# Last layer normalisation of a hybrid attention and mixture-of-experts block: tokens loaded and stored in pairs of tiles

## The reference, cut to what matters

```
def layer_norm(x, g, b):
    xf = x.astype(jnp.float32)
    mu = jnp.mean(xf, -1, keepdims=True)
    var = jnp.mean(jnp.square(xf - mu), -1, keepdims=True)
    y = (xf - mu) * lax.rsqrt(var + LN_EPS)
    return (y * g.astype(jnp.float32) + b.astype(jnp.float32)).astype(x.dtype)
...
    h = layer_norm(DN_ALPHA * h + ffn, ln2_g[l], ln2_b[l])
return h[:, N_META:]
```

## Time and profile before

| what | value |
|---|---|
| median of 3 runs | 2524.76 us (2520.92 to 2529.96) |
| the profiled execution's own time | 2522.01 us |
| its span, first to last instruction | 2519.9 us |
| instructions | 35973 |
| PE busy | 2200.0 us (87%) |
| DVE busy | 1700.5 us (67%) |
| ACT busy | 1504.0 us (60%) |
| POOL busy | 331.3 us (13%) |
| first instruction of `phase_combine` | 2462.9 us after the start of the span |

### The profile page before, as it was taken

How to read it: one execution, slowest core, us unless ns; L and a number is a source line. 1 busy time by engine, 2 the same in 40 slices (tenths; PEclk the granted TensorE clock), 3 DMA queues, 4 the chain that set the end, 5 groups by cost and what they waited for, 6 DMA issues and landing times. The chain is left out here.

```text
span 2519.9 us, 35973 instructions
## 1 busy us (share of the span) xinstructions
PE 2200.0 (87%) x11294; PEld 1783.4 (71%) x11294; DVE 1700.5 (67%) x3112; ACT 1504.0 (60%) x2389; POOL 331.3 (13%) x436
## 2 busy tenths in 40 slices
PE   7999899758859999999979995599999999999970
PEld 6778788635547777777858884487888888888860
DVE  5323231166658888888843333889999999999976
ACT  4323241266646777776743432477888888788866
POOL 0111111100000000000000000112222222222211
PEclk9999999979979999999989997799999999999995
DMA  6425352252252222211043331799878779999837
GB/s 196 174 100 157 121 180 84 75 133 77 68 129 66 66 68 68 68 39 36 9 149 134 145 137 59 255 368 322 270 239 274 251 250 316 326 313 300 272 93 283
DMA packets 210506, 420.06 MB, mean 167 GB/s; under 512 B 36264, under 2 KB 86776, under 8 KB 209496
## 3 DMA queue, kind: packets, MB, share of 16 engines
q1 hardware_dynamic: 177352, 314.15, 36.6%
q0 software_dynamic: 32016, 103.26, 14.2%
q10 hardware_dynamic: 1032, 1.31, 0.4%
HBM read 437.12 MB, written 86.39 MB: 208 GB/s over the span
## 5 line engine op out<-in xcount | busy, mean ns | idle before, releaser
L2343 DVE TENSOR_TENSOR moe_w_lo<-fetch_w_raw,moe_w_hi 128x1024 fp32r<-128x1024 f32 x376 | 435.4, 1218 | 12.1 <-ACT moe_w_hi L2272 11.9
L2272 ACT ACTIVATE moe_w_hi<-fetch_w_raw 128x1024 fp32r<-128x1024 f32 x376 | 369.1, 1053 | 75.7 <-DMA fetch_w_raw<-in_w_e_up_dram 39.2
L2397 PE MATMUL moe_ps_gu<-moe_w_hi,moe_xT_hi 128*128 128x512 f32 x736 | 293.2, 398 | 4.5 <-DVE moe_xT_lo L2354 4.5
L2399 PE MATMUL moe_ps_gu<-moe_w_hi,moe_xT_lo 128*128 128x512 f32 x736 | 288.9, 393 | 0.0
L2398 PE MATMUL moe_ps_gu<-moe_w_lo,moe_xT_hi 128*128 128x512 f32 x736 | 288.5, 392 | 0.0
L1350 ACT ACTIVATE fox_p_hi<-fox_ps_t 128x512 fp32r<-128x512 f32 (+4 forms) x352 | 181.3, 531 | 108.5 <-PE fox_ps_t L1490 107.7
L1417 DVE TENSOR_TENSOR fox_p_lo<-fox_ps_t,fox_p_hi 128x512 fp32r<-128x512 f32 (+4 forms) x352 | 211.0, 611 | 28.8 <-ACT fox_p_hi L1350 27.3
L1490 PE MATMUL fox_ps_t<-ident,fox_s 128*128 128x128 f32 (+1 forms) x1216 | 200.0, 279 | 29.6 <-ACT fox_s L1343 18.7
L2349 DVE TENSOR_TENSOR moe_d_lo<-fetch_d_raw,moe_d_hi 128x1024 fp32r<-128x1024 f32 x184 | 213.0, 1221 | 10.3 <-ACT moe_d_hi L2280 10.1
L1404 DVE CUSTOM_DVE_ANT_0 fox_s<-fox_ps_r,fox_ncum 128x512 f32<-128x512 f32 (+4 forms) x352 | 193.7, 569 | 21.1 <-PE fox_ps_r L1475 14.0
L1343 ACT ACTIVATE fox_s<-fox_s,fox_ntop 128x144 f32<-128x144 f32 (+5 forms) x192 | 173.4, 904 | 46.8 <-DVE fox_ntop L1412 46.4
(11 more groups left out here) (312 smaller groups left out, 5002.9 us busy)
## 6 DMA issues: line engine op xcount, KB each, us to landing
fetch_w_raw<-in_w_e_gate_dram SPq DMA_DIRECT2D x192, 512.0 KB
fetch_w_raw<-in_w_e_up_dram SPq DMA_DIRECT2D x192, 512.0 KB
fetch_d_raw<-in_w_e_down_dram SPq DMA_DIRECT2D x92, 1024.0 KB
proj_w_raw<-in_w_in_dram SPq DMA_DIRECT2D x24, 1024.0 KB, 5.2
proj_xt<-in_x_dram SPq DMA_DIRECT2D x16, 512.0 KB
h<-proj_hrow POOLq DMA_DIRECT2D x16, 512.0 KB, 3.4
win_q_raw<-qT SPq DMA_DIRECT2D x32, 256.0 KB, 4.0
mix_o<-o SPq DMA_DIRECT2D x16, 512.0 KB, 4.4
```

Source lines behind the costliest of these rows:

```text
L2272: nc.scalar.activation(w_hi[:, k], w_raw[:, k].rearrange("p j n -> p (j n)"), ACT.Copy).then_inc(gu_high, 1)
L2343: nc.vector.tensor_tensor(w_lo[:, k], w_raw[:, k].rearrange("p j n -> p (j n)"), w_hi[:, k].bitcast(F32), ALU.subtract).then_inc(gu_split, 1)
L2397: nc.tensor.matmul(out, xT_hi[:, slot, k], w_hi[:, k, cols], start=k == 0, stop=False)
L2399: done = nc.tensor.matmul(out, xT_lo[:, slot, k], w_hi[:, k, cols], start=False, stop=k == KT - 1)
```

## The change

A pair of tiles (2 pair, 2 pair + 1) now has one load and one store of 1 MB instead of two of 512 KB. The slots stay as they were: four of `base` and four of `out`, pair 0 in slots 0 and 1, pair 1 in slots 2 and 3, and so on. SP has 8 loads, POOL 8 stores. The load of a pair waits until both tiles of the pair two before it have passed L2523. The store waits until both its tiles are finished. ACT waits, for either tile of a pair, on the pair's one semaphore, and DVE waits before L2523, for either tile, until the store of the whole pair two before has landed. The work of ACT and DVE on a tile is the same.

```
-        base_in = [m.sem(f"base_in{i}") for i in range(4)]
+        base_in = [m.sem(f"base_in{i}") for i in range(2)]
...
-        stored = [m.pool_dma_sem(f"stored{i}") for i in range(4)]
+        stored = [m.pool_dma_sem(f"stored{i}") for i in range(2)]
...
-            def load(n, slot, use):
-                wait(sp, normed, n - 3)
-                sp.dma_start(base[:, slot], t["acc"][n * P:(n + 1) * P, :]).then_inc(base_in[slot], 16)
-                if n == 0:
+            for pair in range(TILES // 2):
+                two = slice(2 * (pair % 2), 2 * (pair % 2) + 2)
+                wait(sp, normed, 2 * (pair - 1))
+                sp.dma_start(base[:, two], t["acc"][2 * pair * P:2 * (pair + 1) * P, :].rearrange("(j p) d -> p j d", p=P)
+                             ).then_inc(base_in[pair % 2], 16)
+                if pair == 0:
                     sp.dma_start(gain[:], row_broadcast(t["ln2_g"][0], P)).then_inc(const_in, 16)
                     sp.dma_start(shift[:], row_broadcast(t["ln2_b"][0], P)).then_inc(const_in, 16)
-
-            tiles(sp, load)
...
-            def store(n, slot, use):
-                pool.wait_ge(ready, n + 1)
-                pool.dma_start(t["out"][0, n * P:(n + 1) * P, :], out[:, slot]).then_inc(stored[slot], 16)
-
-            tiles(pool, store)
-            for i in range(4):
+            for pair in range(TILES // 2):
+                two = slice(2 * (pair % 2), 2 * (pair % 2) + 2)
+                pool.wait_ge(ready, 2 * (pair + 1))
+                pool.dma_start(t["out"][0, 2 * pair * P:2 * (pair + 1) * P, :].rearrange("(j p) d -> p j d", p=P),
+                               out[:, two]).then_inc(stored[pair % 2], 16)
+            for i in range(2):
                 pool.wait_ge(stored[i], 16 * TILES // 4)
...
-                act.wait_ge(base_in[slot], 16 * (use + 1))
+                act.wait_ge(base_in[slot // 2], 16 * (use + 1))
...
-                wait(dve, stored[slot], 16 * use)
+                wait(dve, stored[slot // 2], 16 * use)
```

## The result

The changed kernel takes 2533.5 us (median of 7 runs, 2528.98 to 2539.05) against 2524.76 us before. The ratio of the runs is 1.0034, with a 95% interval of 1.0020 to 1.0047. It is slower, by 8.7 us or 0.34%; 2534.0 was predicted. The interval reaches from 5 to 12 us, so the runs show that there is a loss, and not its size to a microsecond. The profiled execution took 2530.75 us, its span is 2528.7 us.

The account below looks back on a forecast made before the run. Last phase taken as lead-in, sixteen tiles at 2.64 us with ACT and DVE in step and DMA busy, lead-out. 1.55 + 6.3 + 0 + 1.35 = +9.2 us on 2524.76 made 2534.0; range 2527.7, rounded down, to 2541.

Parts of the forecast that it names:

- Part 1: Start of last phase: tile 0 waits for 1.049 MB, so ACT starts tile 1 later, +1.55 us (1.1 to 1.75).
- The cover of gain and shift: Start of last phase: gain and shift usable 1.5 us before DVE asks for them after ACT's root of tile 0.
- Part 2: Middle: pair loads take 5.9 us against 3.81 allowed, stalling ACT before pairs 2, 4, 6; +6.3 us (3.3 to 9.6).
- Part 2's aside on the size: Middle: half of each pair asks 2.64 us later and twice as much must come in the time left.
- Part 3: DVE's wait for stores before L2523: stores take 6.4 us against 7.4 us available, so it costs nothing.
- Part 4: End of last phase: last store moves 1.049 MB, +1.28 us, and POOL's issue +0.07; +1.35 us (1.28 to 1.5).
- Part 5: Vanished SP and POOL issues are worth nothing; tail with four fewer semaphores to reset, 0 to -0.3 us, taken 0.
- Busy all the time at 410 GB/s: Last phase before the change: the 16 DMA engines are always busy, leaving no rate for larger transfers to win.
- The pair's load nearly in time: First rival, ACT's L2505 of tiles 4, 8, 12: load takes 4.66 us, +5.4 us in sum; chance 0.23.
- Transfers queued one behind the other: Second rival, middle: loads take 7.5 us and DVE waits for stores too, sum 14.0 us; chance 0.14.
- The pattern of two pieces: Third rival, pair transfers: not spread over 16 engines, moving at half rate or below, about +21 us; chance 0.03.

Follow-up runs that it names:

- the kernel without stores: Changed kernel without the stores of pairs 0 to 6 and DVE's wait for them, output incomplete; phase 61.6 us, middle 46.0 us.
- The late-release run: Single 512 KB tiles as before, but both loads of a pair issued only at the pair's release point; ratio to before 1.0035, phase 65.5 us.
- the trimmed kernel: Kernel before, with root table loaded early, tile 1 loaded ahead of shift, last tile finished and stored in halves; ratio 0.9995, phase 55.7 us.
- pairs with eight slots: Changed kernel with eight input and eight output slots instead of four each; ratio to before 1.0014, phase 58.7 us.

## Why the prediction was right

The sum was +9.2 us on the profiled execution; it measured +8.7, of which 8.4 lie in the last phase. The medians, 2534.0 predicted and 2533.5 measured, agree more closely than they can tell: the interval of the ratio is 7 us wide, and the same kernel's phase measured +7.6 us in its second profile. The terms were off by -1.0, +0.7 and -0.5 us, and that they partly cancel is luck; that the middle carries the loss, by loads that miss ACT, is not. By its own steps:

**Part 1, the first load: the place was right, the size was not.** +1.55 us was predicted, with 1.1 as the lower bound; +0.58 was measured, below both. The step that failed is the reading of the stretches. I took the time at which 1.049 MB in total had moved as the time at which the pair's megabyte would be through, and assumed the same rates after the change: 270 GB/s until 2468. After the change, the stretch 2466 to 2468 runs at 418 GB/s and only the next at 317 (share and GB/s last):

```profile
2466.00:2468.00 2.00, 0.00 (x0) 0.00 (x0) 0.00 (x0) 0.00 (x0) 0.00 (x0) 0.50 1.04 418
2468.00:2470.00 2.00, 0.00 (x0) 0.00 (x0) 0.00 (x0) 1.44 (x3) 0.00 (x0) 0.50 0.96 317
```

In both kernels the slow stretch is the one in which the gain row should be on its way, the transfer behind the first load; that it is slow because all 128 copies read one row is a guess, which no run tested. These rates are about half of the error. The rest is the time from the pair's last data to ACT, some 0.8 us, where 1.1 to 1.5 had been taken. Tile 0 was late by 0.84 us instead of 1.7. Further, tile 1 started 0.26 us sooner behind tile 0 than before (3.94 us against 4.20), because its data were there; of that I had counted 0.17. The start also varies: ACT started tile 1 at 8.9 to 9.5 us in the seven profiles with a first pair and at 8.5 to 8.9 us in the five with single tiles, so the cost is about 0.5 us, and below 1.1 in any case. The cover of gain and shift held: DVE's first reciprocal is released by ACT's root alone.

**Part 2, the pair's load: right in size and in cause, wrong in the pattern.** The six late loads took 5.13, 6.69, 6.39, 4.99, 5.24 and 6.62 us from issue to ACT's start, 5.84 on average, against 5.9 predicted and 3.81 allowed. The two parts of the 5.9 were tested apart: 4.9 alone (4.80 measured) and 1.0 for the store beside it (1.0 on average). Three loads lie on the path, as said: 6.67 + 4.97 + 6.60 less 3 x 3.81 is 6.8 us, where 6.3 was predicted. What failed is "before pairs 2, 4 and 6, not before 3, 5 and 7". This holds only if all loads take equally long, as in the kernel without stores. As the loads of pairs 3 and 7 took 1.6 and 1.4 us longer than those before them, they missed ACT once more, and the path went through pairs 3, 5 and 7.

What makes them unequal can be counted in the packets of the trace, 256 of 4 KB for each pair's load or store. The data of the six loads moved in 3.75, 4.90, 5.04, 3.59, 3.85 and 4.94 us, and in these times 55, 140, 181, 37, 47 and 156 store packets started. Without stores it was 3.27 to 3.57 us. Over the 18 such loads of the change, its repeat and the kernel without stores, the time is 3.4 us and 9.4 ns more for each store packet (correlation 0.98). So the 1.0 us for the store was right as a mean: 103 packets are 0.42 MB, 1.0 us at 410 GB/s. Its working was not. The data of the first six stores started 2.5 to 2.7 us after the issue, where 1.1 was taken, and for pairs 3, 4, 5 and 7 the store one pair earlier was still moving when the load's data began. In the 4.9 us, too, two errors cancel: alone, a pair's data moved at 290 to 320 GB/s and not at 410, and ACT started 0.4 us behind it and not about 1.

**Part 2's aside on the size was half wrong.** It named two causes at once, the late release and twice the data. The late-release run shows that the first alone gives a loss of 8.3 us where stores share the engines; the second adds 2.8 beside single stores.

**Part 3, the stores: right, but with less to spare than it looked.** DVE did not wait for a store. Yet in the change the six stores landed only 0.3 to 0.4 us before the L2523 that needed them, and one of its repeat 0.05 us before, where 7.4 - 6.4 = 1.0 us had been worked out. (The rival that prices this wait is the second, not the third.) With the cover gone the wait appears, 4.7 us in three places (paired stores alone) and 7.4 us in four (eight input slots). The 6.4 us taken for a store's time were too few: 5.4 us that DVE leaves plus the wait of 1.6 make 7.0.

**Part 4, the last store: the data as predicted, the end shorter.** The issue on POOL took 0.71 us instead of 0.53 (+0.18, inside 0 to 0.21), and the data twice as long, 2.76 us instead of 1.43; the time from the last data to the end fell by 0.66 us. So +0.82 instead of +1.35.

**Part 5** bounded that tail by -0.3 us and named the wrong cause, the semaphores. It fell by 0.66 us, by the wait of POOL that the last section shows.

**What bounds the phase.** "Busy all the time at 410 GB/s" rested on one stretch. Early in the middle, the kernel before has stretches of 2 us at 307, 406 and 201 GB/s (2476 to 2482), and keeps to 354 GB/s or more only from 2482 to 2508. ACT and DVE keep their step there too; what the sum took from the row is the rate of 410, which a load alone didn't reach (part 2).

**The rivals.** The pair's load nearly in time (+5.4 us) fell on 5.84 us against 4.66. By the Trainium skill (DMA: Bandwidth & Descriptors, section Anatomy of one DMA, SWDGE path) a megabyte would take an estimated 4.4 us; the fit is for transfers that GpSimd issues, and SP issues these. The load with nothing beside it took 4.80 here, and the measurement decides. The rule of the same page's section Bandwidth, to batch to 1 MiB, won nothing here, as the 512 KB transfers already ran at 410 GB/s. Transfers queued one behind the other (+14 us) came near in the kernel with paired loads alone (+11.7 us of phase, loads of 7.4 us on average), though there without a wait of DVE for stores, and not in the change. The pattern of two pieces spreads as the single one does: 418 GB/s.

## What to carry to other kernels

When a ring of slots stays the same and its transfers double, the release of half the slots moves later by one step of the work; compare the time from that release to the consumer's need with the time that a transfer takes beside the others, on the load's side and on the store's, before asking what the larger transfer saves. A stall on one side is the cover of the other: with more input slots alone nothing was won, and only room on both sides removed the loss. A chain that is already full on two engines can't pay anything back, so every stall there counts in full.

## What the runs showed of the hardware

At the end of the phase, when its last store has landed, POOL runs one DRAIN instruction, and the program ends 1.0 us after it. This DRAIN takes longer the more DMAs POOL has issued in the phase. The rows (ns min/median/max, start us), for the kernel before with 16 such DMAs, the change with 8, the pairs with hardly any stores with 1, and the trimmed kernel with 17:

```profile
L2444 POOLq DRAIN  x1: 1365/1365/1365, 2517.6 to 2517.6; - x1
L2444 POOLq DRAIN  x1: 711/711/711, 2527.0 to 2527.0; - x1
L2444 POOLq DRAIN  x1: 139/139/139, 2524.7 to 2524.7; - x1
L2444 POOLq DRAIN  x1: 1447/1447/1447, 2518.8 to 2518.8; - x1
```

The other kernels fit: 217 ns with 2 DMAs, 788 with 9, 711 to 719 in all six executions with 8 and 1365 in all three with 16, about 82 ns for each. That is nearly the whole difference in the tail: 0.65 of the 0.66 us between the kernel before and the change. In the stretches, the last one in which nothing moves is 2.9 us in the kernel before and 2.2 in the change; with one store and with seventeen it is (GB/s last):

```profile
2524.10:2525.70 1.60, 0.00 (x0) 0.00 (x0) 0.00 (x0) 0.00 (x0) 0.00 (x0) 0.50 0.00 0
2518.10:2521.20 3.10, 0.00 (x0) 0.00 (x0) 0.00 (x0) 0.00 (x0) 0.00 (x0) 0.50 0.00 0
```

It isn't the number of semaphores: pairs with eight slots have as many as the kernel before, and 719 ns. It isn't the bytes either, since eight stores of 1 MB move as much as sixteen of 512 KB. What POOL does in the DRAIN, no run shows.

A second finding is the low rate with busy DMA engines: stretches of 2 us with a DMA share of 1.06 at 248 GB/s stand beside others of 1.02 at 382 and 1.00 at 410. It is not bound to loads meeting stores, since the start of the kernel before, where no store has been issued, has 0.99 at 270. Its cause stays open. In the change and its repeat, the waits trade places mainly with the number of store packets that fall into a load, as counted above; in the kernel with paired loads alone, two loads (pairs 5 and 6) took 2.1 and 1.6 us more than that count gives.
